# Taking four more down-projection pages apart into high and low parts in a routed-expert stage

## What is computed

```python
    for e in range(N_EXPERTS):
        hid = jax.nn.silu(t @ w_gate[e]) * (t @ w_up[e])
        out = out + combine[:, e:e + 1] * (hid @ w_down[e])
```

## Time and profile before

| | us |
|---|---|
| median of 3 runs (1963.02 to 1965.69) | 1963.66 |
| the profiled execution | 1963.64 |
| its span, first to last instruction | 1961.9 |
| PE busy | 1896.5 |
| POOL busy | 1254.8 |

### The profile page before, as it was taken

How to read it: one execution, slowest core, us unless ns; L and a number is a source line. 1 busy time by engine, 2 the same in 40 slices (tenths; PEclk the granted TensorE clock), 3 DMA queues, 4 the chain that set the end, 5 groups by cost and what they waited for, 6 DMA issues and landing times.

```text
span 1961.9 us, 34620 instructions
## 1 busy us (share of the span) xinstructions
PE 1896.5 (97%) x14058; PEld 1729.9 (88%) x14058; DVE 972.0 (50%) x2112; ACT 772.5 (39%) x860; POOL 1254.8 (64%) x299
## 2 busy tenths in 40 slices
PE   7989899999997999999999999999999999999998
PEld 5779788877663999999999797999999999999998
DVE  3766455666645466546335636433353334743112
ACT  4443344344412455335333524433343334334332
POOL 6717167857610777878874241577768786858874
PEclk9999899999998999999999999999999999999999
DMA  9637167788899566665665222466646664756552
GB/s 366 247 113 295 46 279 298 280 319 340 348 392 384 212 235 218 234 244 210 251 255 198 105 89 84 152 256 235 228 193 257 228 251 181 278 186 217 188 175 85
DMA packets 64105, 448.81 MB, mean 229 GB/s; under 512 B 7824, under 2 KB 8944, under 8 KB 9968
## 3 DMA queue, kind: packets, MB, share of 16 engines
q1 hardware_dynamic: 62032, 441.85, 59.1%
q10 hardware_dynamic: 1952, 5.24, 0.7%
HBM read 446.01 MB, written 1.05 MB: 228 GB/s over the span
## 4 chain that ended last, share of the span: by engine, by line
PE 64%; issue 17%; POOL 10%; DMA 3%; DVE 3%; ACT 1%; SPq 0%; POOLq 0%; DVEq 0%; ACTq 0%
PE bank L801 14%; PE bank L803 14%; PE bank L802 14%; POOL W L711 10%; PE bank L1405 3%; PE bank L1333 3%; PE bank L1334 3%; PE bank L1340 3%; DMA raw<-in_pages 2%; PE bank L827 2%; DVE XR L2174 1%; DMA mraw<-in_mpages 1%; PE bank L1253 1%; PE bank L1312 1%; PE bank L836 1%
## 5 line engine op out<-in xcount | busy, mean ns | idle before, releaser
L711 POOL TENSOR_TENSOR W<-raw,W 128x2048 fp32r<-128x2048 f32 x219 | 1010.4, 4618 | 537.3 <-ACT W L1725 536.5
L801 PE MATMUL bank<-YH,W 128*128 128x256 f32 x1920 | 546.9, 285 | 1.3 <-POOL W L711 0.8
L803 PE MATMUL bank<-YH,W 128*128 128x256 f32 x1920 | 543.2, 283 | 0.0
L802 PE MATMUL bank<-YL,W 128*128 128x256 f32 x1920 | 543.1, 283 | 0.0
L1725 ACT ACTIVATE W<-raw 128x2048 fp32r<-128x2048 f32 x218 | 416.2, 1910 | 300.0 <-PE bank L803 273.4
L801 PEld LDWEIGHTS bank<-YH,W 128*128 128x128 f32 x1920 | 367.9, 192 | 4.7 <-POOL W L711 1.6
L802 PEld LDWEIGHTS bank<-YL,W 128*128 128x128 f32 x1920 | 368.2, 192 | 0.4 <-issue 0.2
L803 PEld LDWEIGHTS bank<-YH,W 128*128 128x128 f32 x1920 | 368.1, 192 | 0.0
L2122 DVE SCALAR_TENSOR_TENSOR bank<-mraw,CA,bank 128x256 f32<-128x256 f32 x696 | 328.9, 488 | 19.8
L2220 DVE TENSOR_TENSOR bank<-bank,SIL 128x256 f32<-128x256 f32 x110 | 47.5, 432 | 531.9 <-ACT SIL L1744 531.9
L801 PE MATMUL bank<-HH,W 128*128 128x256 f32 x880 | 249.7, 284 | 1.7 <-DVE HL L2222 1.3
(11 more groups left out here) (411 smaller groups left out, 2927.4 us busy)
## 6 DMA issues: line engine op xcount, KB each, us to landing
raw<-in_pages SPq DMA_DIRECT2D x274, 1024.0 KB, 4.8
mraw<-in_mpages SPq DMA_DIRECT2D x98, 1024.0 KB, 6.9
R<-in_pages SPq DMA_DIRECT2D x20, 1024.0 KB, 7.5
XR<-in_pages SPq DMA_DIRECT2D x12, 1024.0 KB, 5.8
W6F<-in_pages SPq DMA_DIRECT2D x10, 1024.0 KB, 15.3
R<-in_mpages SPq DMA_DIRECT2D x4, 1024.0 KB, 16.1
HT<-in_acts ACTq DMA_DIRECT2D x1, 1024.0 KB, 14.2
CT<-in_mpages SPq DMA_DIRECT2D x1, 1024.0 KB, 19.0
```

Source lines behind the costliest of these rows:

```text
L711: nc.gpsimd.tensor_tensor(WL[:, p % SLOTS, :], raw[:, p % SLOTS, :], WH[:, p % SLOTS, :].bitcast(f32), ALU.subtract).then_inc(s_lo, 1)
L801: mm(out, w[0], x[0], start=start, stop=False, skip_group_check=True)
L802: mm(out, w[0], x[1], start=False, stop=False, skip_group_check=True)
L803: return mm(out, w[1], x[0], start=False, stop=stop, skip_group_check=True)
```

## The change

The down pages of units 16, 18, 20 and 22 (the even ones of slot 3) are taken apart too. Their high part goes to `RR[:, 0:2048]`, the place of slot 2's token operand (the third pair `XG[2]`), whose last reader is unit 15. Their low part is written by POOL over the page. The four slow matmuls of these units become twelve fast ones; the hidden values get a high and a low part.

```diff
--- before.py
+++ after.py
@@ -291,14 +291,16 @@
         PS = [ctx.enter_context(nc.psum_tensor(f"bank{b}", [P, 512], f32)) for b in range(8)]
         ACC, GU, MODB, MISC = (0, 1, 2, 3), (4, 5), 6, 7
         TURN = 4
-        SPLIT_DOWN = range(1, NE8)
+        SPLIT_DOWN = list(range(1, NE8)) + list(range(2 * NE8, WHOLE, 2))
         SPLIT_JOBS = [t for t in range(NJOB) if JOBS[t][0] in SPLIT_DOWN]
         HTH, HTL = HH[:, :, 0:P], HL[:, :, 0:P]
+
+        XG_FLAT = [RR[:, j * D:(j + 1) * D] for j in range(2)]
 
         def down_high(u):
             if u % 2:
                 return [CTR[:, j * D:(j + 1) * D] for j in range(2)]
-            return list(OS[0])
+            return list(OS[0] if u < NE8 else XG_FLAT)
 
         def down_low(u):
             low = XRR if u % 2 else RR[:, 6144:6144 + PAGE]
@@ -769,7 +771,7 @@
                     p_.tensor_tensor(PAIRL[u % 2][:, part].rearrange("p k n -> p (k n)"), expert_raw(u, part),
                                      PAIRH[u % 2][:, part, :].bitcast(f32), ALU.subtract).then_inc(s_mlo, 1)
                 if u - 1 in SPLIT_DOWN:
-                    pool.wait_ge(sem("expert_down_high"), u - 1)
+                    pool.wait_ge(sem("expert_down_high"), SPLIT_DOWN.index(u - 1) + 1)
                     for j in range(2):
                         last = p_.tensor_tensor(down_low(u - 1)[j], down_page(u - 1)[:, j * D:(j + 1) * D],
                                                 down_high(u - 1)[j].bitcast(f32), ALU.subtract)
@@ -1379,12 +1381,13 @@
                         pe.wait_ge(s_osl, 2 if slot_j == 2 else 2 * slot_j)
                 if u in SPLIT_DOWN:
                     pe.wait_ge(sem("hidden_low"), SPLIT_JOBS.index(t) + 1)
-                    pe.wait_ge(sem("expert_down_low"), u)
+                    pe.wait_ge(sem("expert_down_low"), SPLIT_DOWN.index(u) + 1)
                     wh, wl = down_high(u), down_low(u)
                     for j in range(2):
                         for n in range(2):
                             o, cols = PS[out_banks(slot_j)[n]][:, :], slice(n * 512, (n + 1) * 512)
-                            mm(o, HTH[:, j, :], wh[j][:, cols], start=False, stop=False, skip_group_check=True)
+                            mm(o, HTH[:, j, :], wh[j][:, cols], start=(u % NE8 == 0 and j == 0), stop=False,
+                               skip_group_check=True)
                             mm(o, HTL[:, j, :], wh[j][:, cols], start=False, stop=False, skip_group_check=True)
                             last = mm(o, HTH[:, j, :], wl[j][:, cols], start=False, stop=(u % NE8 == NE8 - 1 and j == 1),
                                       skip_group_check=True)
@@ -1943,7 +1946,7 @@
                     gathered_hi(2, 1)
                     expert_split(1, 0)
                     expert_split(1, 1)
-                if j == 0 and u in SPLIT_DOWN:
+                if DONE_AT[u] == t + (u < NE8) and u in SPLIT_DOWN:
                     down_split(u)
                 if DONE_AT[u] == t and u + 2 < WHOLE:
                     expert_split(u + 2, 0)
```

## The result

| | before | after |
|---|---|---|
| median | 1963.88 us (20 runs, 1961.1 to 1967.86) | 1967.12 us (20 runs, 1963.45 to 1970.74) |
| ratio | | 1.0015, 95% interval 1.0009 to 1.0022 |
| profiled execution, span | 1961.9 us | 1964.1 us |

The change makes the kernel 3.2 us slower. The forecast was 1965.5 us, 1.9 us longer than before, with a range of 1961.9 to 1968.2 us.

The account below looks back on a forecast made before the run. PE was taken to bound units 16 to 23, then the DMA page stream; 1.7 us saved, all given back plus 1.9 us at the gather: 1963.64 + 1.9 = 1965.5 us, range 1961.9 to 1968.2 us.

Parts of the forecast that it names:

- the gather follows without a wait: Sign of being wrong: PE's gather of slot 4's tokens (L1255) shows no idle time ahead, where 1 us or more was forecast.
- the single L2492 of over 4 us: Sign of being right: DVE's `onehot` instruction L2492 shows once with more than 4 us, ending near 544 us.
- The load into `XR`: Load of unit 23's down page, starting the page stream; issued at 553.84 us before, forecast near 555.7 us.
- The chain at unit 20: `hidden_low` delays `onehot`, POOL's later page of unit 22 holds it, and the gather of slot 4's tokens starts 1.9 us late.
- the hold on `onehot`: DVE's `onehot` stands still while POOL instructions are in progress; its matrix is ready only at about 544.4 us.
- the wait at the gather: PE's gather of slot 4's tokens, at 542.46 us before, waits for `onehot` and starts 1.9 us late.
- unit 21's second page in time: Issued at 522.4 instead of 517.6 us, it must land by 528.3 us for POOL; landing 2.4 us later would be in time.
- the port's lock: DVE and POOL share an exclusive port lock, held for the whole instruction by whichever of `tensor_scalar` and GpSimd operation starts first.
- I cost them at nothing: ACT's two added copies per unit, 2.1 us, come behind the unit's SiLU while the next page is on its way.
- POOL becomes the bound: Rival, chance 0.20: unit 21's second page lands at 530.9 us, POOL's sequence is 2.6 us later; +4.5 us, 1968.1 us.
- the 1.7 us saved: Fast matmuls in `down` save PE 0.58 us a unit, 1.7 us for the three units ahead of 553.84 us.
- Unit 16: `out_low` follows `hidden_low`, so `down` starts 0.9 us later; with 0.6 us saved, PE is some 0.3 us late.

Follow-up runs that it names:

- e2: The changed kernel with ACT's copy of unit 21's second page moved behind its copy of unit 19's hidden values; median 1968.21 us, ratio 1.0016.
- e11: The kernel before with the change for unit 20 alone; median 1965.07 us, ratio 1.0009.
- e8: The changed kernel with DVE's half page of unit 20 held back until POOL's page of unit 20 is written; median 1965.66 us, ratio 1.0007.
- e4: The kernel before with the change for units 16 and 22 alone; median 1964.33 us, ratio 1.0004.
- e3: The kernel before plus POOL's idle subtractions, which `down` of units 16, 18, 20 and 22 waits for; slow matmuls kept; median 1966.76 us, ratio 1.0017.
- e6: The changed kernel with the low parts of the four down pages written by DVE instead of POOL; median 1965.85 us, ratio 1.0010.

## Why the prediction was right, and where not

**The number.** It lies in the range, and that is in part luck. The prediction had named as a sign of being wrong that the gather follows without a wait, and in both traces of the changed kernel it does; the single L2492 of over 4 us is missing there too. The wait that costs the time stands one unit earlier, at a place that the forecast did not have.

**Right.** PE bounds units 16 to 23 and the page stream what follows; the fast matmuls save 0.6 to 0.7 us a unit; waits that end at a time PE does not set take more than that back; the stream starts later and the end with it. The load into `XR` was forecast for 555.7 us and came at 558.55 us, 0.7 us of it the later start.

```profile
558.55 0.33 SPq L664 DMA_DIRECT2D XR<-in_pages  x1
```

The chain at unit 20 is real where unit 19's wait does not hide it (e2, e11), and so is the hold on `onehot`.

**The step that failed** is the one that put the wait at the gather and called unit 21's second page in time. PE waited 3.60 us ahead of unit 19's `down` and not at all at the gather. I asked of that page only when POOL would want it (landing by 528.3 us) and not who stands behind its copy on ACT. The copy of unit 19's hidden values stood there, and PE wanted it earlier than POOL wanted the page. Its issue was forecast for 522.4 us and came at 525.06 us: 0.7 us are the shift of the whole trace, and 2.1 us POOL's page being held by DVE. The prediction named the port's lock for whichever comes first, and costed it one way only, POOL holding DVE; e8 has the other way at 2.1 us. The "I cost them at nothing" for ACT's copies was right about the added copies, and missed what a late page does there. The rival "POOL becomes the bound" had the late page, but made late by a slow landing (8.5 us) and felt through POOL: the page took 4.8 us to land, was issued late, and was felt on PE through ACT.

**The sum, as measured**, by the start of each `down` from that of unit 15 on, in us (start of the stage taken off):

| | before | after | longer by, since the row above |
|---|---|---|---|
| unit 16 | 9.59 | 9.19 | -0.40 |
| unit 17 | 20.23 | 19.42 | -0.41 |
| unit 18 | 29.90 | 29.54 | 0.45 |
| unit 19 | 40.42 | 43.25 | 3.19 |
| unit 20 | 50.08 | 54.72 | 1.81 |
| the gather | 54.33 | 58.28 | -0.69 |

(The starts are read from PE's timeline.) The last column adds up to 3.95 us, the stage's 3.9. The row of unit 19 holds the wait of 3.60 us less unit 18's saving, that of unit 20 the slow clock: from unit 19's `down` to the scatter behind it (L1281 at 536.94) PE took 4.8 us instead of 3.0. The row of unit 18 holds a wait of 0.18 us and no saving; the other 0.27 us of it stay open. The forecast of +1.9 us was a wait of 3.6 us at the gather less the 1.7 us saved. So its wait had the right size at the wrong place, by luck, and the clock was not in it.

**Unit 16** was forecast 0.3 us late and was not: no trace of the changed kernel has a wait ahead of its `down`. The repeat of the kernel before has none either, so the 0.27 us of the earlier trace rows and the long gap in ACT's work ahead of it belong to that execution, and not to the kernel. e4 says that unit 16 costs nothing.

**Left open.** Why the profiled execution of the change is only 2.2 us longer with a stage 3.9 us longer is in the last section; how often each outcome at the port falls in the unprofiled runs is not known. Units 16 and 22 alone are no slower than before, and no faster by what 11 runs can tell. No version here beats the kernel before.

## What to carry to other kernels

Work moved to an engine with idle time is not free when what it does next frees a buffer: ask for the load that waits for it, then for every instruction behind the one that waits for that load. Where two engines lock each other out at a port, the lock delays either of them: DVE lost 3.4 us in one order (5.65 us for 2.28), POOL 2.1 us in the other (6.67 for 4.6). In four traces DVE stood ready while POOL subtracted, and came ahead of POOL's next page. Put a wait between them, or keep such pairs out of the stretch where one of them frees pages. A wait of PE is to be priced with the matmuls behind it, which may run at the lower clock.

## What the runs showed of the hardware

The granted clock stood at 1.00 while PE waited ahead of unit 19's `down` in the changed kernel, fell to 0.50 about a microsecond after PE had begun again, and was back at 1.00 from 537 us. In the repeat it fell shortly before PE began again, and was at 0.50 from 535 to 541 us. Two waits of under 1 us each in e11 were followed by some 7 us at the lower clock; waits of 1.28 and 0.78 us in e8 were not followed by a slow gather (2.00 us for it, 2.84 in e11). The length of one wait does not decide it: behind 2.24 us in e3 the `down` took 5.40 us, and behind 2.92 us in e6 the clock stayed at 1.00:

```profile
520.00:525.00 5.00, 4.29 (x25) 3.81 (x26) 4.96 (x9) 1.64 (x1) 0.00 (x0) 1.00 0.80 283
```

I cannot say from these runs what decides.

The same shows at the end of the page stream, where PE waits 3.8 us in every trace. The eight matmuls behind that wait, before and after:

```profile
636.47 3.68 PE L1398 MATMUL bank<-R,WRT 128*64 128x512 f32 x8 [3.82 <-ACT WRT L1890]
...
641.14 1.94 PE L1401 MATMUL bank<-R,WRT 128*64 128x512 f32 x8 [3.81 <-ACT WRT L1893]
```

They took 3.68 us in both executions of the kernel before, and 1.94 us in this one of the changed kernel (3.68 in its repeat; 2.77 to 3.68 in the experiments). From the end of the stage to the first modulation sum of the next one (L2120 at 656.33 us before, L2123 at 658.46 us after and at 664.86 us in the repeat) were 51.5 us before, 49.0 us after, and 51.4 us in the repeat. So the profiled execution of the change got 2.5 us back which its repeat did not, 1.7 of them in these eight matmuls. How often that happens in the unprofiled runs, the times do not tell.
